# The up projection of the second block as seven block products, with the weights standing and 128 token columns moving, and a convolution that reads from SBUF

## The reference, cut to what matters

```
def conv_glu(x, w_up, conv_w, conv_b, w_down):
    hid = x @ w_up                      # 256 x 1024 by 1024 x 5632
    hid = causal depthwise convolution of width 3 along the tokens, + conv_b
    gate, up = hid[..., :2816], hid[..., 2816:]
    return (silu(gate) * up) @ w_down
```

## Time and profile before

| | us |
|---|---|
| median of 3 runs (lowest, highest) | 1623.03 (1622.95, 1627.83) |
| profiled execution, its own time | 1621.46 |
| its span, first to last instruction | 1619.7 |
| PE busy, share of the span | 1542.2, 95% |
| POOL busy, share of the span | 290.6, 18% |

### The profile page before, as it was taken

One profiled execution on the slowest core, in us unless ns is written; L12 is line 12 of the kernel. 1 busy time (PEld: TensorE's weight loads), 2 busy tenths in 40 slices (PEclk: granted clock), 3 DMA queues, 4 the chain that ended last, 5 costly groups with the idle time before them and its releaser, 6 DMA issues.

```text
span 1619.7 us, 25135 instructions
## 1 busy us (share of the span) xinstructions
PE 1542.2 (95%) x10304; PEld 1123.6 (69%) x10304; DVE 785.3 (48%) x1623; ACT 375.0 (23%) x896; POOL 290.6 (18%) x296
## 2 busy tenths in 40 slices
PE   3999989999999989999999999999999989999999
PEld 3455556666655566777878888874788764788887
DVE  5889944454589977574880101012533322233322
ACT  2222243243312223223321000000214441311100
POOL 4013330000003313000110000002575200000264
PEclk9999999999999999999999999999999999999999
DMA  9846670230496545766772444443543123444441
GB/s 323 230 157 195 240 255 1 50 111 11 158 304 223 190 144 163 277 244 240 289 277 99 156 156 156 156 168 118 201 172 130 53 105 104 145 148 148 147 177 68
DMA packets 171193, 270.86 MB, mean 167 GB/s; under 512 B 51021, under 2 KB 84920, under 8 KB 169800
## 3 DMA queue, kind: packets, MB, share of 16 engines
q1 hardware_dynamic: 145840, 201.08, 36.6%
q0 software_dynamic: 16512, 42.49, 8.2%
q10 hardware_dynamic: 8728, 25.69, 4.2%
HBM read 226.16 MB, written 42.99 MB: 166 GB/s over the span
## 4 chain that ended last, share of the span: by engine, by line
PE 87%; DVE 5%; DMA 3%; ACT 2%; issue 2%; POOL 0%; DVEq 0%; ACTq 0%; SPq 0%; POOLq 0%
PE bank L481 83%; PE bank L484 5%; DMA memory<-in_w_mod 1%; DMA memory<-mc_scratch 1%; DMA memory<-in_mla_w_in 1%; ACT memory L1427 0%; DVE memory L2276 0%; DVE memory L2283 0%; DVE memory L2277 0%; DVE memory L2280 0%; DVE memory L2424 0%; DVE memory L2392 0%; DVE memory L2403 0%; ACT memory L1706 0%; DVE memory L2114 0%
## 5 line engine op out<-in xcount | busy, mean ns | idle before, releaser
L481 PE MATMUL bank<-memory 128*128 128x256 f32 (+10 forms) x9476 | 1454.0, 355 | 51.6 <-DMA memory<-in_w_mod 8.1
L481 PEld LDWEIGHTS bank<-memory 128*128 128x128 f32 (+4 forms) x9476 | 1030.9, 159 | 436.2 <-issue 266.7
L2589 POOL TENSOR_TENSOR memory<-memory 128x1024 f32<-128x1024 f32 (+1 forms) x16 | 36.9, 2306 | 600.6 <-DMA memory<-in_w_in 278.9
L484 PEld LDWEIGHTS bank<-memory 128*128 128x128 f32 (+1 forms) x828 | 94.3, 141 | 55.5 <-issue 29.4
L484 PE MATMUL bank<-memory 128*128 128x128 f32 (+1 forms) x828 | 109.3, 276 | 21.9 <-ACT memory L1271 9.0
L2550 POOL DMA_DIRECT2D mc_scratch<-memory x32 | 28.0, 876 | 508.0 <-DVE memory L1999 449.8
L2556 POOL DMA_DIRECT2D k_scratch<-memory x128 | 76.4, 631 | 14.0 <-ACT memory L1344 13.6
L2459 DVE SCALAR_TENSOR_TENSOR memory<-bank,memory 128x255 f32<-128x255 f32 x44 | 21.0, 478 | 98.3 <-ACT memory L1738 98.3
L2325 DVE TENSOR_SCALAR memory<-bank,memory 128x256 f32<-128x256 f32 x16 | 6.6, 476 | 112.3 <-PE bank L481 112.3
L2114 DVE TENSOR_REDUCE memory<-bank 128x1 f32<-128x512 f32 (+1 forms) x48 | 30.2, 684 | 63.6 <-PE bank L481 63.6
L2332 DVE TENSOR_TENSOR memory<-memory 128x256 f32<-128x256 f32 x16 | 6.7, 419 | 105.8 <-ACT memory L1607 105.8
(11 more groups left out here) (278 smaller groups left out, 1069.2 us busy)
## 6 DMA issues: line engine op xcount, KB each, us to landing
memory<-in_s_w_glu SPq DMA_DIRECT2D x16, 2048.0 KB, 8.9
memory<-in_w_mod SPq DMA_DIRECT2D x12, 2048.0 KB, 14.1
memory<-in_w_ffn_up SPq DMA_DIRECT2D x22, 1024.0 KB, 6.6
memory<-in_w_in SPq DMA_DIRECT2D x10, 2048.0 KB, 7.7
mc_scratch<-memory POOLq DMA_DIRECT2D x32, 512.0 KB, 4.4
mb_scratch<-memory ACTq DMA_DIRECT2D x32, 512.0 KB, 3.6
memory<-mb_scratch SPq DMA_DIRECT2D x32, 512.0 KB, 7.4
memory<-mc_scratch POOLq DMA_DIRECT2D x32, 512.0 KB, 6.5
```

The lines of the kernel that those rows point to most:

```text
L481: return nc.tensor.matmul(o, l, r, start=start, stop=stop, skip_group_check=free)
L484: return nc.tensor.transpose(o, i, ident[0:n, 0:n])
L2589: nc.gpsimd.tensor_tensor(t1, b12, b11, ALU.subtract).then_inc(*S.up("w_sum", (key, 1)))
```

## The change

Each step of the up projection becomes seven block products. The tile's quarters are upper or lower half of the 1024 rows, and first or second 128 columns, of gate and up alike (`up_quarters`). A product is 2 x 4 matmuls, with 128 x 128 weights standing and 128 tokens (or one of their sums) moving, so a step has 56 matmuls of 128 columns in place of 32 of 256. POOL makes the weight sums of all eleven tiles; tile f + 2 waits for product 4, the last one, of step f, since the buffers of sums are two. ACT and DVE put the products together into a new SBUF buffer `hid`, two steps deep: ACT copies products 1 and 1 + 5 out (`up_u1`, `up_a5`; from step 2 on both after product 5) and then the finished first quarter (`up_c11`), DVE does five additions (`up_out`). The convolution's three taps then read `hid` in place of the banks.

From step 2 on PE's order is product 1 (`up_first`), 5, 7, 6 (`up_middle`), 2 (`up_second`), 3, 4 (`up_last`). Product 2 waits for `up_u1` and `up_a5` of its own step, product 4 for `up_u2`. Steps 0 and 1 start with products 1 and 2 of both, since these need the tokens' first half alone.

```diff
-            load(("up", f), None, (2, KD, 256), ("up_mm", (f, 1)), parts)
+            load(("up", f), None, (2, KD, 256), ("product", (("up", f), 4)), parts)
...
+            def up_product(o, w, v, start, stop):
+                for half in range(2):
+                    for k in range(4):
+                        last = mm(o[:, half * P:(half + 1) * P], w[:, half, k, :], v[:, k, :], start and half == 0 and k == 0,
+                                  stop and half == 1 and k == 3, True)
...
+                pe.wait_ge(*S.at("up_u1", f))
+                if f > 1:
+                    pe.wait_ge(*S.at("up_a5", f))
+                up_product(b[0][:, 0:T], b21, h2[:, 4:8, 0:P], False, True).then_inc(*S.up("product", (("up", f), 2)))
...
+                pe.wait_ge(*S.at("w_sum", (("up", f), 4)))
+                pe.wait_ge(*S.at("up_u2", f))
+                up_product(b[1][:, 0:T], t4, h2[:, 4:8, P:T], False, True).then_inc(*S.up("product", (("up", f), 4)))
...
+            hn_turned(1, 0)
+            up_first(0)
+            hn_turned(1, 1)
+            up_second(0)
+            up_first(1)
+            up_second(1)
+            for f in range(2):
+                up_middle(f)
+                up_last(f)
...
+            rms(1, 1)
+            up_part("up_u1", 0, 1, 0)
+            hn_scaled(1, 1)
+            up_part("up_u1", 1, 1, 0)
             for f in range(KF // 2):
+                if f > 1:
+                    up_part("up_u1", f, 5, 0)
+                up_part("up_a5", f, 5, 1)
...
-                        A(cg[:, n, half, :], at_bank("up", f, half)[:, i * T:(i + 1) * T], ACT.Identity,
+                        A(cg[:, n, half, :], hid[:, f % 2, half, i, :], ACT.Identity,
...
+            dve.wait_ge(*S.at("hnT", (1, KD - 1, 1)))
+            left_sums(in_sums, h2[:, 0:4, 0:P], h2[:, 4:8, 0:P], h2[:, 0:4, P:T], h2[:, 4:8, P:T], "up_sum", (1, 3, 2, 4))
...
-                        b = at_bank("up", f, half)[:, i * T:(i + 1) * T]
+                        b = hid[:, f % 2, half, i, :]
...
+            for f in range(KF // 2):
+                b11, b12, b21, b22 = up_quarters(weights(pool, ("up", f), (2, KD, 256)))
+                t1, t2, t4 = up_sums(f)
+                if f >= 2:
+                    pool.wait_ge(*S.at("product", (("up", f - 2), 4)))
+                nc.gpsimd.tensor_tensor(t1, b12, b11, ALU.subtract).then_inc(*S.up("w_sum", (("up", f), 1)))
...
```

More of the change, by code:

```diff
@@ L102 @@
           "v7": "unit_op", "u2": "unit_op", "c22": "unit_op", "c12": "unit_op", "c21": "unit_op", "in_sum": "unit_op", "down_sum": "unit_op",
+          "up_u1": "unit_act", "up_a5": "unit_act", "up_c11": "unit_act", "up_v7": "unit_op", "up_u2": "unit_op", "up_c22": "unit_op",
+          "up_c12": "unit_op", "up_c21": "unit_op", "up_sum": "unit_op",
           "down_x": "unit_op", "down_u1": "unit_act", "down_a5": "unit_act"}
@@ L346, in build @@
         down_parts = take(2, 6, T)
+        hid = take(2, 2, 2, T)
         st2 = small[:, 64:128]
@@ L430, in quarters, with up_quarters, up_sums @@
             return w[:, 0:kk, 0:256], w[:, 0:kk, 256:512], w[:, kk:2 * kk, 0:256], w[:, kk:2 * kk, 256:512]
+        def up_quarters(w):
+            return w[:, :, 0:4, 0:P], w[:, :, 0:4, P:2 * P], w[:, :, 4:8, 0:P], w[:, :, 4:8, P:2 * P]
+        def up_sums(f):
+            return [down_w_sums[:, f % 2, i, :].rearrange("p (h k n) -> p h k n", h=2, k=4) for i in range(3)]
         def weight_sums(key):
@@ L436, in weight_sums @@
             kk = 3 if key[2] == 2 else 4
-            return [down_w_sums[:, key[1], i, 0:256 * kk].rearrange("p (k n) -> p k n", k=kk) for i in range(3)]
+            return [down_w_sums[:, (key[1] + KF // 2) % 2, i, 0:256 * kk].rearrange("p (k n) -> p k n", k=kk) for i in range(3)]
         def in2_out(ct, t, half):
@@ L1200, in _ @@
                     last.then_inc(*S.up("out2_mm", (n, t)))
[L1201 to L1204, removed]
+            up_banks = {}
+            def up_product(o, w, v, start, stop):
                 for half in range(2):
[L1206 to L1224, removed]
+                    for k in range(4):
+                        last = mm(o[:, half * P:(half + 1) * P], w[:, half, k, :], v[:, k, :], start and half == 0 and k == 0,
+                                  stop and half == 1 and k == 3, True)
@@ new lines, in up_product, with up_first, up_second @@
+                return last
+            def up_first(f):
+                up_banks[f] = b = bank(pe, ("up", f, 0), [("up_c12", f)]), bank(pe, ("up", f, 1), [("up_c21", f)])
+                b11, _, _, _ = up_quarters(weights(pe, ("up", f), (2, KD, 256)))
+                pe.wait_ge(*S.at("hnT", (1, 3, 0)))
+                up_product(b[0][:, 0:T], b11, h2[:, 0:4, 0:P], True, False).then_inc(*S.up("product", (("up", f), 1)))
+            def up_second(f):
+                b = up_banks[f]
+                _, _, b21, _ = up_quarters(weights(pe, ("up", f), (2, KD, 256)))
+                pe.wait_ge(*S.at("hnT", (1, 7, 0)))
+                pe.wait_ge(*S.at("up_u1", f))
+                if f > 1:
+                    pe.wait_ge(*S.at("up_a5", f))
+                up_product(b[0][:, 0:T], b21, h2[:, 4:8, 0:P], False, True).then_inc(*S.up("product", (("up", f), 2)))
@@ new lines, in up_last @@
+            def up_last(f):
+                b = up_banks[f]
+                _, _, _, b22 = up_quarters(weights(pe, ("up", f), (2, KD, 256)))
+                _, _, t4 = up_sums(f)
+                pe.wait_ge(*S.at("up_sum", 4))
+                pe.wait_ge(*S.at("up_a5", f))
+                up_product(b[0][:, T:2 * T], b22, in_sums[:, 3], False, True).then_inc(*S.up("product", (("up", f), 3)))
+                pe.wait_ge(*S.at("w_sum", (("up", f), 4)))
+                pe.wait_ge(*S.at("up_u2", f))
+                up_product(b[1][:, 0:T], t4, h2[:, 4:8, P:T], False, True).then_inc(*S.up("product", (("up", f), 4)))
@@ L1225, in _ @@
+            hn_turned(1, 0)
[7 more added lines that the diff above has]
+                up_last(f)
+            for f in range(2, KF // 2):
+                up_first(f)
+                up_middle(f)
+                up_second(f)
+                up_last(f)
             down_banks = {}
@@ L1726, in _, with up_part @@
                 A(mT[:, 2 * k2:2 * k2 + 2, :], at_bank("mT", k2).rearrange("p (k t) -> p k t", k=2), ACT.Copy).then_inc(*S.up("mT", k2))
-            for t in range(2):
-                rms(1, t)
-                hn_scaled(1, t)
-            for f in range(KF // 2):
+            def up_part(name, f, i, o):
+                act.wait_ge(*S.at("product", (("up", f), i)))
+                if f >= 2:
+                    act.wait_ge(*S.at("up_u2", f - 2))
+                A(in2_parts[f % 2][:, o, :], at_bank("up", f, 0)[:, o * T:(o + 1) * T], ACT.Copy).then_inc(*S.up(name, f))
+            rms(1, 0)
+            hn_scaled(1, 0)
+            rms(1, 1)
+            up_part("up_u1", 0, 1, 0)
+            hn_scaled(1, 1)
+            up_part("up_u1", 1, 1, 0)
+            for f in range(KF // 2):
+                if f > 1:
+                    up_part("up_u1", f, 5, 0)
+                up_part("up_a5", f, 5, 1)
+                act.wait_ge(*S.at("product", (("up", f), 3)))
+                if f >= 2:
+                    act.wait_ge(*S.at("conv", (f - 2, 1, 1)))
+                A(hid[:, f % 2, :, 0, 0:P], at_bank("up", f, 0)[:, 0:T].rearrange("p (h n) -> p h n", h=2), ACT.Copy).then_inc(*S.up("up_c11", f))
+                act.wait_ge(*S.at("up_c11", f))
+                act.wait_ge(*S.at("up_c21", f))
                 for half in range(2):
@@ L2450, in _, with up_out @@
                 rms(1, t)
+            dve.wait_ge(*S.at("hnT", (1, KD - 1, 1)))
+            left_sums(in_sums, h2[:, 0:4, 0:P], h2[:, 4:8, 0:P], h2[:, 0:4, P:T], h2[:, 4:8, P:T], "up_sum", (1, 3, 2, 4))
+            two = lambda v: v.rearrange("p (h n) -> p h n", h=2)
+            def up_out(f):
+                part, b = in2_parts[f % 2], [at_bank("up", f, i) for i in range(2)]
+                dve.wait_ge(*S.at("product", (("up", f), 6)))
+                dve.wait_ge(*S.at("up_a5", f))
+                tt(part[:, 3, :], b[1][:, 0:T], part[:, 1, :], ALU.add).then_inc(*S.up("up_v7", f))
+                tt(part[:, 2, :], b[1][:, T:2 * T], part[:, 0, :], ALU.add).then_inc(*S.up("up_u2", f))
+                dve.wait_ge(*S.at("up_u2", f))
+                if f >= 2:
+                    dve.wait_ge(*S.at("tap2", (f - 2, 1, 1)))
+                tt(hid[:, f % 2, :, 1, P:T], two(part[:, 2, :]), two(part[:, 3, :]), ALU.add).then_inc(*S.up("up_c22", f))
+                dve.wait_ge(*S.at("product", (("up", f), 3)))
+                dve.wait_ge(*S.at("up_c11", f))
+                tt(hid[:, f % 2, :, 1, 0:P], two(b[0][:, T:2 * T]), two(part[:, 2, :]), ALU.add).then_inc(*S.up("up_c12", f))
+                dve.wait_ge(*S.at("product", (("up", f), 4)))
```

(3 more changed lines are left out.)

22 lines of the change are left out of this document (20 added, 2 removed).

## The result

The change makes the kernel slower. The median is 1682.06 us (1679.15 to 1683.37, 4 runs) against 1622.99 (1621.96 to 1627.83, 4 runs) of the kernel before: a ratio of 1.0355, 95% interval 1.0339 to 1.037. The direction and the wait are those of the prediction; the price of the wait is not, and the time lies 6 us above the predicted range.

A forecast was written before the change was run, and what follows sets the result against it. PE, busy without waits in the up stage, was taken as the bound. Step 1's end at 1430.7, nine steps of 17.05 and late token sums put the stage's end at 1586.7, +37.6 us: 1660 us, range 1628 to 1676.

The forecast's parts named there:

- PE's own work: Up stage: a step of seven products takes PE 12.72 us (12.50 to 12.95) against 13.82, if it never waits.
- What a step waits for: Up stage: product 2 waits for ACT's copies behind DVE's taps, one tap per POOL instruction; a step lasts 17.05 us.
- rival of dearer views: POOL's sums on new views take 0.3 us more an instruction, a step 1.2 more: 1671; chance 0.13, shared with the low clock.
- pairs that slip through: Rival: one POOL instruction lets two convolution taps pass, product 2 starts at E + 9.1; +16, 1639 us; chance 0.14.
- taps that don't wait: Rival: convolution taps run unhindered beside POOL, steps last 12.72 us; -3.9, 1619 us; chance 0.12.
- the walk: Timing of one up step: POOL's four sums end by E + 10.1, copies by E + 11.55, product 4 at E + 17.05.
- the 1664: Time if, by the skill page's wording, three POOL instructions a step were set back 0.15 each, nine steps by 4 us.
- E: The time at which product 4 of step f, the step's last product in the up stage, ends.
- PE starts product 2 at E + 11.6 and does 2, 3, 4 in 5.45 us: Up step: product 2 starts at E + 11.6 in place of 7.3, and the three products end at E + 17.05.
- The low clock: Rival: products after PE's wait run at 1.2 GHz in half the steps, 27 us more, 1687; chance 0.13, shared with dearer views.
- The token sums: After steps 3 and 7 DVE makes four token sums, about 2.7 us; product 4 starts 1.25 late twice.
- The start: Step 0 of the up stage: PE waits 1.6 us for the second half's norm; five products end the step at 1415.1.

## Why the prediction was right in kind and short in size

- **PE's own work** (12.72 a step): right. Unhindered it is 12.53.
- **What a step waits for**: right, one tap behind each POOL instruction. POOL's instruction on its new views takes 2.41, so the rival of dearer views falls; so do the pairs that slip through (1639) and the taps that don't wait (1619). POOL's four instructions take 9.82 us together (1456.47 to 1466.29), where the walk had 9.85, so nothing of the 1664 shows either. Product 2 starts at E + 11.37, predicted 11.6.
- **"PE starts product 2 at E + 11.6 and does 2, 3, 4 in 5.45 us"**: this term failed. It priced the 48 MATMULs at the full clock. In steps 2 to 9 they took 6.96 to 8.53 us, 7.64 in the mean of eight pieces of the chain, 2.2 more. What the runs showed in its place is products granted 0.64 to 0.80 behind PE's wait. Nine times 2.2, less nine times the 0.23 by which product 2 came earlier and the 2.5 of the next point, is 15.2 of the 15.5 missed. The run with PE kept busy confirms the cause: 5.61 and 17.00. The low clock was among the rivals, as half of the steps at half speed (1687; half of nine steps of 5.45 is 24.5 us, not the 27 put down); I gave it too little chance although showed 0.83 in a stage that idles. It isn't an alternative to the wait: it came with each of the nine, and belonged in the sum. The 0.8 of step 1 has the same cause, 5.29 us for 32 MATMULs behind its wait.
- **The token sums** (twice 1.25): they cost nothing in the changed kernel, since products 2 and 3, slowed, end later than `up_u2` comes. Where the clock was full the two sets cost 1.26 and 1.25.
- **The start** (20.6): 3.6 short. I let the scaling of the second half run free, though POOL's sums of tile 1 wait for nothing but their tile and lie beside it; that is 1.8 us. Another 1.6 is the clock again, 5.22 us for the 32 MATMULs behind PE's wait against 3.59 with POOL's sums later. The first token sum was slowed too, but PE did not wait for it. The Trainium skill (SBUF — State Buffer, "Who interferes with whom") also lists `tensor_scalar` among the operations that can enter a two-port mode and then contend with GpSimd. The scaling is one, with one SBUF input, 2.58 us beside POOL and 0.75 without; the prediction's account of one SBUF input left this exception out.
- **The rest of the program**: the down projection is unchanged, as predicted: from the last product of the up stage to the end of the span 70.4 us (1609.19 to 1679.6), before 70.6 (1549.1 to 1619.7). The 2.6 us ahead of the stage stay open. In the ten profiles of this study the first scaled block starts between 1394.48 and 1399.14 without an order that follows an edit; the kernels with POOL's sums have both early and late ones (1394.76 and 1397.10). They are there long before the stage: the piece of 88 MATMULs of 17.92 us in the part ahead starts at 1226.85 in the changed kernel and at 1224.21 before, and the runs of the kernel before differ by more (1621.96 to 1627.83). No run was made on it.

## What to carry to other kernels

When work is moved to an engine that was idle, list every instruction of the neighbour engine that now runs beside it and has both operands in SBUF, and the TENSOR_SCALAR with its one (2.58 against 0.75 us here), those at the stage's start too; one operand in PSUM, or another place in the order, can be the whole difference (59 us here, and a kernel 0.8% faster than before in the end). When a change makes TensorE wait inside a dense stage, price the products behind the wait at a lowered clock too, and not only at the pace of the dense stage. And when work is moved into a gap, take the gap's start from what the instruction ahead of it waits for, not from when its engine is free.

## What was not expected of the hardware

- A wait of 4.24 us in a step of 19 brought the products behind it to a granted 0.64 to 0.80, and one of 2.85 in a step of 17.1 brought the one product behind it to 0.55. In both kernels the products ahead of the wait ran at 1.00.
- 36 more MATMULs a step, with results that nobody reads, made the kernel 18.6 us faster (1682.06 to 1663.44). From the first scaled block to the end of the span it is 266.3 us (1394.90 to 1661.2) against 282.5 (1397.10 to 1679.6), so 16.2 of it lie here, and they come through the clock: product 2 still waited for the same copy and started at E + 11.39, against 11.37.
